# A two-layer hybrid backbone: gated expert outputs added by the scatter to the residual in DRAM, and narrow products turned round

## The chip, the cores and the metric

The kernel runs on one core of one Trainium2 chip, in fp32. The metric is the device time of one execution in microseconds. The change is judged by the median of several executions, before against after.

## What is computed

One inference step of a two-layer backbone over 640 tokens (128 context, 512 latent) of 1024 features. Layer 0 is attention beside a convolution, layer 1 a gated DeltaNet; behind each stands a hierarchical mixture of 16 experts, of which every token uses two. Each half layer is added to the residual x after multiplication by a gate row. There are two gate rows, one for context tokens and one for latent tokens. Cut to what matters here:

```python
def hier_moe(h, w_gr, b_gr, w_er, b_er, w_gate, w_up, w_down):
    t = h.reshape(b * l, d)
    g_logits = (t @ w_gr).astype(F32)                  # 4 groups
    e_logits = (t @ w_er).astype(F32)                  # 16 experts
    ...                                                # one group, two experts in it, weights e_w
    combine = jnp.sum(jax.nn.one_hot(expert, N_EXPERTS) * e_w[..., None], 1)
    hid = jax.nn.silu(jnp.einsum('td,edf->tef', t, w_gate)) * jnp.einsum('td,edf->tef', t, w_up)
    out = jnp.einsum('tef,efd->td', hid * combine[..., None], w_down)
# in the layer: x = x + gate_row * hier_moe(modulate(rms_norm(x, g), shift, scale))
# DeltaNet: proj = h @ w_in, whose last 32 columns are the gates (beta and decay)
```

## The kernel before

The five token tiles of 128 stand in SBUF as X. Five engines run their own instruction lists: PE (TensorE), DVE (VectorE), ACT (ScalarE), POOL (GpSimd) and SP, which issues the weight loads. Semaphores join them.

**Output projection and logits** (`out_pe`, `out_act`, `out_dve`, once a layer). PE projects ten half tiles (L973). From the seventh on, it also transposes the normalised rows of a tile that is ready (L985), which ACT copies to hT, and multiplies them by the 20 router columns (L992): per tile eight products with hT as the weights of 128 columns, of which only 20 columns are streamed. Each fp32 product is two instructions. POOL stores the normalised rows to h2d in DRAM.

**Routing** (`route_dve`, `route_pe`) gives each of the 1280 (token, expert) pairs a slot. There are 16 expert tiles of 128 slots and a loop over extra tiles, which runs at least once, so that 17 tiles are worked off in each layer here. The result is two index lists: tokens to gather, and rows of y2d (two rows per token) to scatter to. Free slots point at 256 padding rows.

**Experts** (`moe_*`). For tile t, POOL gathers 128 rows of h2d (L1326, 512 KB). PE transposes them (L1378), runs gate and up (L1386, 64 instructions), transposes tile t+1, and then runs down (L1397). ACT takes the silu, and DVE multiplies into the hidden tile (L1450). The down result is copied from PSUM to one of two buffers yb, half by ACT and half by DVE (L1426, `y_copy`), and POOL scatters it to y2d (L1330, 512 KB). Before each gather and each scatter POOL runs a one-column multiplication and a drain (`gate`, L1322). POOL's order is gather t+4, scatter t, gather t+5, scatter t+1, and so on, to the gather of tile 16; after that come scatters alone. The copy of tile t waits until the scatter of tile t-2 has landed, since it takes its buffer. DVE's order is hidden t, transposed rows of t+1, copy t, hidden t+1. SP loads 3 MB of weights per tile, four tiles ahead.

**Combination** (`comb_*`). When everything has landed, SP loads both rows of each token from y2d (L1475 and L1476, ten loads of 512 KB). ACT multiplies one by its weight (L1480). DVE adds the other by its weight (L1484), multiplies by the gate row (L1487) and adds to X (L1489). In layer 0 each tile then goes through the next norm: ACT squares (L1494) and takes a root, DVE scales (L421), PE transposes (L456), and ACT modulates eight 128x128 blocks (L400) into hT. Behind it `gates_pe` multiplies hT by the 32 gate columns (L1615): 40 products, 80 instructions, with 32 columns streamed. In layer 1 X is stored to the outputs (L2375).

## Time and profile before

| | us |
|---|---|
| median of 3 runs | 1771.22 |
| lowest, highest | 1764.03, 1777.72 |
| the profiled execution | 1759.8 |
| its span in the trace | 1757.9 |
| PE busy | 1476.2 (84%) |
| DVE, ACT, POOL busy | 744.2, 508.0, 178.6 |
| DMA moved | 268.09 MB, mean 153 GB/s |

The profiled execution is 11.4 us below the median. The page lists busy time by engine, by 40 slices of the span, and by groups of instructions; an idle time in a group stands with what ended it ("<-"). A row of the timeline is start, duration, engine, line, operation, output from inputs, and in brackets the idle time ahead of it and its releaser. "PEclk" is the granted TensorE clock as a share of 2.4 GHz: 1.00 is 2.4 GHz, 0.50 is 1.2 GHz. A DMA's row on POOL or SP is the time of issuing it. The time from issue to landing is listed apart.

### The profile page before, as it was taken

The numbers are of one execution on the slowest core, as the hardware profiler recorded it, in microseconds if no ns is written. First come the engines' busy times: TensorE is split into PE (matmuls) and PEld (weight loads), VectorE is DVE, ScalarE is ACT, GpSimd is POOL, SyncE is SP. The second block draws the span as 40 slices with busy tenths as digits, with TensorE's granted clock in tenths as the row PEclk, the third lists the DMA queues.
The fourth block names the chain that finished last, engine by engine and source line by source line (L and its number), as shares of the span: only waits on it lengthen the run. The fifth ranks groups of instructions, "written<-read, shape, count | busy, mean of one in ns | idle before, by whom it ended". The sixth has DMA issues, their size and how long they took to land.

```text
span 1757.9 us, 33612 instructions
## 1 busy us (share of the span) xinstructions
PE 1476.2 (84%) x14556; PEld 1070.3 (61%) x14556; DVE 744.2 (42%) x1420; ACT 508.0 (29%) x1115; POOL 178.6 (10%) x249
## 2 busy tenths in 40 slices
PE   3999669979869989368989999989989996899892
PEld 2556357754558767265767767767755445787671
DVE  0375867632421111233655556566645435111114
ACT  2202334440201101254544545445432111111011
POOL 3000020010011111102101101110100000211120
PEclk8999689999869999758988899999999996899996
DMA  9413774522469985522011112012013315698845
GB/s 359 161 51 131 243 251 149 189 63 107 172 236 329 342 294 195 208 71 62 29 42 39 39 42 58 21 42 70 5 54 130 113 72 203 227 349 295 277 173 210
DMA packets 166260, 268.09 MB, mean 153 GB/s; under 512 B 7408, under 2 KB 106912, under 8 KB 165600
## 3 DMA queue, kind: packets, MB, share of 16 engines
q1 hardware_dynamic: 150720, 210.32, 35.8%
q0 software_dynamic: 15392, 55.61, 8.6%
q8 instruction: 115, 1.88, 0.5%
q14 instruction: 33, 0.27, 0.0%
HBM read 237.93 MB, written 27.98 MB: 151 GB/s over the span
## 4 chain that ended last, share of the span: by engine, by line
PE 53%; issue 21%; DVE 9%; DMA 6%; ACT 4%; POOLq 3%; DVEq 2%; POOL 1%; SPq 0%; ACTq 0%; PEldq 0%
PE psum L1746 8%; PE psum L973 7%; PE psum L541 4%; PE psum L1808 3%; POOLq L1323 3%; DMA ring<-in_w_mod 3%; PE psum L1386 3%; PE psum L311 2%; PE psum L821 2%; PE psum L1758 2%; PE psum L2305 2%; PE psum L527 2%; PE psum L800 2%; DMA arena<-in_w_mod 1%; PE psum L1397 1%
## 5 line engine op out<-in xcount | busy, mean ns | idle before, releaser
L1746 PE MATMUL psum<-hT,ring 128*128 128x384 f32 (+1 forms) x768 | 257.0, 461 | 2.0 <-ACT modN L1976 1.6
L1746 PEld LDWEIGHTS psum<-hT,ring 128*128 128x128 f32 x768 | 136.7, 197 | 39.7 <-issue 3.9
L1386 PEld LDWEIGHTS psum<-arena,ring 128*128 128x128 f32 x1152 | 134.0, 195 | 12.0 <-issue 9.6
L1386 PE MATMUL psum<-arena,ring 128*128 128x128 f32 x1152 | 134.8, 279 | 3.7 <-DVE arena L1420 3.7
L1426 DVE COPY arena<-psum 128x512 f32<-128x512 f32 x34 | 23.5, 692 | 240.7 <-DMA y2d<-arena,small 192.3
L673 DVE SCALAR_TENSOR_TENSOR arena<-arena,params_sb 128x655 f32<-128x655 f32 x120 | 106.3, 913 | 4.8
L1808 PEld LDWEIGHTS psum<-arena 32*32 32x32 f32 x5120 | 55.8, 110 | 69.6 <-issue 41.7
L1808 PE MATMUL psum<-arena 32*32 32x32 f32 x5120 | 65.1, 200 | 32.5 <-issue 21.9
L1426 ACT COPY arena<-psum 128x512 f32<-128x512 f32 x34 | 19.9, 586 | 244.9 <-DMA y2d<-arena,small 207.5
L1397 PE MATMUL psum<-ring,arena 128*128 128x512 f32 x144 | 71.6, 644 | 15.2 <-DVE arena L1450 15.2
L1397 PE MATMUL psum<-modN,arena 128*128 128x512 f32 x128 | 60.7, 619 | 12.2 <-DVE arena L1450 12.2
L541 PE MATMUL psum<-hT,ring 128*128 128x512 f32 (+1 forms) x256 | 70.3, 435 | 0.7 <-ACT modN L604 0.7
L973 PE MATMUL psum<-ring,hT 128*128 128x512 f32 x160 | 69.6, 594 | 1.2 <-ACTq L208 1.2
L973 PE MATMUL psum<-ring,arena 128*128 128x512 f32 x160 | 69.6, 594 | 1.2 <-ACTq L208 1.2
L1450 DVE TENSOR_TENSOR arena<-arena,psum 128x256 f32<-128x256 f32 x34 | 14.3, 421 | 127.5 <-PE psum L1386 125.1
L1386 PEld LDWEIGHTS psum<-arena,hT 128*128 128x128 f32 x512 | 58.4, 192 | 3.8 <-issue 3.8
L1386 PEld LDWEIGHTS psum<-arena 128*128 128x128 f32 x512 | 58.4, 192 | 3.8 <-issue 3.8
L541 PEld LDWEIGHTS psum<-hT,ring 128*128 128x128 f32 x256 | 38.9, 191 | 32.6 <-issue 32.6
L1386 PE MATMUL psum<-arena 128*128 128x128 f32 x512 | 58.5, 275 | 0.0
L1386 PE MATMUL psum<-arena,hT 128*128 128x128 f32 x512 | 58.5, 275 | 0.0
L1397 PEld LDWEIGHTS psum<-ring,arena 128*128 128x128 f32 x144 | 28.2, 206 | 46.2 <-issue 30.3
L1032 DVE TENSOR_TENSOR arena<-psum,modG 128x512 f32<-128x512 f32 x20 | 13.8, 691 | 94.9 <-PE psum L973 94.9
(419 smaller groups left out, 2598.9 us busy)
## 6 DMA issues: line engine op xcount, KB each, us to landing
ring<-in_w_mod SPq DMA_DIRECT2D x24, 1024.0 KB, 5.3
ring<-in_m_w_gate SPq DMA_DIRECT2D x18, 1024.0 KB, 6.6
ring<-in_m_w_up SPq DMA_DIRECT2D x18, 1024.0 KB, 9.9
ring<-in_m_w_down SPq DMA_DIRECT2D x18, 1024.0 KB, 8.3
arena<-in_w_mod SPq DMA_DIRECT2D x16, 1024.0 KB, 5.4
modN<-in_m_w_down SPq DMA_DIRECT2D x16, 1024.0 KB, 9.7
ring<-in_c_w_in SPq DMA_DIRECT2D x24, 512.0 KB, 7.0
arena<-y2d SPq DMA_DIRECT2D x20, 512.0 KB, 6.9
```

What stands on the lines that cost most here:

```text
L311: m = pe.matmul(out[32 * j:32 * j + 2, :], cond[:, k, :], w[:, c0:c0 + P], start=(k == 0), stop=(k == KC - 1))
L527: m = pe.matmul(bank(t % 2, LAT), hT[:, k, tok(t)], ring[:, 0, k * LAT:(k + 1) * LAT], start=(k == 0), stop=(k == KC - 1))
L541: m = pe.matmul(out, ring[:, s, c0:c0 + P], hT[:, k, o:o + n], start=(k == 0), stop=(k == KC - 1))
L673: m = dve.scalar_tensor_tensor(out=acc[:, fc, :], in0=src, scalar=conv_w(fc, k), in1=acc[:, fc, :], op0=ALU.mult, op1=ALU.add)
L800: m = pe.matmul(bank(b, n0), qT[0:QK, h, tok(qt)], kT[0:QK, h, k0 * P:k0 * P + n0], start=True, stop=True)
L973: m = pe.matmul(bank(n % 4), lhs[:, k, tok(t)], ring[:, OUT_SLOT[l][nb], k * 512:(k + 1) * 512], start=(k == 0), stop=(k == KC - 1))
L1323: pool.drain()
L1386: m = pe.matmul(bank((2, 4)[half] + (1, 3)[half] * q, P, f * P), gu_slot[s][:, c0:c0 + P], xgT[:, q, k, :], start=(k == 0), stop=(k == KC ...
L1397: m = pe.matmul(bank(5 + nb), hidT[:, q, k, :], dn_slot[s][:, k * D + nb * 512:k * D + nb * 512 + 512], start=(k == 0), stop=(k == 1))
L1426: copy(yb[:, q, half * 512:(half + 1) * 512], bank(5 + half)).then_inc(S(f"moe{l}_y"), 1)
L1746: m = pe.matmul(bank(un % 2, w), ring[:, s, c0k:c0k + P], hT[:, k, o:o + w], start=(k == 0), stop=(k == KC - 1))
L1808: m = pe.matmul(bank(b, 32, 32 * i)[QD(q), :], lhs(5 * g + i, q), rhs(5 * g + i, q), start=True, stop=True)
```

## The change

Five things are changed.

1. The residual goes to DRAM. When X is complete ahead of the experts, SP stores it to a new tensor x2d (one DMA, 2.6 MB, on SP's queue ahead of the loads of down weights 2 and 3). The scatter of an expert tile does not write to y2d but adds to x2d (`compute_op=ALU.add`). Since a token has two experts, a scatter waits until the one before it has landed, and the first waits until X is stored.
2. The weight and the gate row move to the expert tile. Routing makes one list (the token row) and two weights per slot: one for a context token and one for a latent token, of which one is zero. DVE builds a gate tile G from the two gate rows (`gate_of`, one tensor_scalar and one scalar_tensor_tensor over 128x1024), and multiplies both halves of the down result by it from PSUM (`y_gated`). ACT has no part in it any more.
3. The combination goes. In layer 0 SP loads the five tiles of X back from x2d. In layer 1 SP copies x2d to the two outputs, DRAM to DRAM.
4. The router logits and the DeltaNet gates are turned round (`narrow_rows`): the 32 narrow columns are the weights and the 128 tokens of hT are streamed. The eight feature blocks go in turn to four groups of 32 output partitions. The result is copied to SBUF, and one product with stacked 32x32 identities adds the four groups and transposes (`logits`, `gate_columns`). The gates go in between the transposes of the next norm.
5. In that norm DVE modulates four of the eight blocks (`modulate_dve`), as it did in the first norm. Two more pad stores of 512 KB, to x2d, stand at the start of POOL's list.

```diff
             for r in range(0, NPAD, P):
                 pool.dma_start(h2d[T + r:T + r + P, :], pad[:]).then_inc(S("pad_stored"), 16)
+                pool.dma_start(x2d[T + r:T + r + P, :], pad[:]).then_inc(S("pad_stored"), 16)
...
+        def modulate_dve(dve, l, t):
+            dve.wait_ge(S("norm_tr"), l * 4 * NT + 2 * t + 2)
+            for j in range(4):
+                k, c = 4 + j, cond_of(t)
+                m = dve.tensor_scalar(hT[:, k, tok(t)], bank(2 + (2 * t + 1) % 4, P, j * P),
+                                      mcol[:, l, 1, k, c:c + 1], mcol[:, l, 0, k, c:c + 1], ALU.mult, ALU.add)
+            m.then_inc(S("in_hT_dve"), 1)
...
+        def narrow_rows(pe, out, w_of, t):
+            for k in range(KC):
+                j = k % 4
+                m = pe.matmul(out[32 * j:32 * j + 32, :], w_of(k), hT[:, k, tok(t)], start=(k < 4), stop=(k >= 4))
+            return m
...
+            def logit_rows(t):
+                pe.wait_ge(S("norm_hT"), l * 2 * NT + 2 * t + 2)
+                if t >= 1:
+                    count_wait(pe, "lg_ev", l * NT + t)
+                first = PARAM_AT["w_r"][0] + l * KC * LGC
+                w = lambda k: params[:, first + k * LGC:first + k * LGC + 32]
+                narrow_rows(pe, bank(7, P), w, t).then_inc(S("lg_mm"), 1)
             def logits(t):
-                pe.wait_ge(S("norm_hT"), l * 2 * NT + 2 * t + 2)
-                for k in range(KC):
-                    w = (l * KC + k) * LGC
-                    m = pe.matmul(bank(7, LGC, t * 32), hT[:, k, tok(t)], PRM("w_r")[:, w:w + LGC], start=(k == 0), stop=(k == KC - 1))
-                return m
+                count_wait(pe, "lg_ev", l * NT + t + 1)
+                return pe.matmul(bank(7, LGC, 256 + t * 32), rows[:, t, :], C("eye32")[:, 0:LGC], start=True, stop=True)
             for n in range(2 * NT):
                 project(n)
                 t = n - NT
                 if t >= 1:
                     h_to_features(t - 1)
+                if t >= 3:
+                    logits(t - 3)
                 if t >= 2:
-                    logits(t - 2)
+                    logit_rows(t - 2)
+            logits(NT - 3)
+            logit_rows(NT - 2)
+            h_to_features(NT - 1)
             logits(NT - 2)
-            h_to_features(NT - 1)
+            logit_rows(NT - 1)
             logits(NT - 1).then_inc(S("rt_by_pe"), 1)
...
+            def logit_copy(t):
+                count_wait(act, "lg_mm", l * NT + t + 1)
+                act.copy(rows[:, t, :], bank(7, P)).then_inc(S("lg_ev"), 1)
...
-            dve.tensor_tensor(LBx[:, :, 0, :], LBx[:, :, 2, :], rep(C("row_id"), LT, 2), ALU.mult)
-            for k in range(2):
-                m = dve.tensor_tensor(LBx[:, k * NT:(k + 1) * NT, 1, :], LBx[:, k * NT:(k + 1) * NT, 2, :], rep(C("row_id")[:, 0:NT], LT, 2), ALU.mult)
-            m.then_inc(S("rt_by_dve"), 1)
+            dve.tensor_tensor(LBx[:, :, 1, :], LBx[:, :, 2, :], rep(wk.rearrange("p k t -> p (k t)"), LT, 2), ALU.mult)
+            dve.tensor_tensor(LBx[:, :, 0, :], LBx[:, :, 2, :], rep(C("row_id"), LT, 2), ALU.mult).then_inc(S("rt_by_dve"), 1)
...
+            dve.tensor_scalar(w_cond[:, 0, :], idxf, float(SEQ), None, ALU.is_lt)
+            dve.tensor_copy(w_slot, bank(6, LT, LT))
+            dve.drain()
+            dve.tensor_tensor(w_cond[:, 0, :], w_cond[:, 0, :], w_slot, ALU.mult)
+            dve.drain()
+            dve.tensor_tensor(w_cond[:, 1, :], w_slot, w_cond[:, 0, :], ALU.subtract)
...
             sp.wait_ge(S("norm_h"), (2 * l + 2) * NT)
+            sp.dma_start(x2d[0:T, :].rearrange("(t p) d -> p t d", p=P), X[:, :, :]).then_inc(S("x_stored"), 16)
...
             def scatter(idx, q):
-                pool.indirect_dma_start(out=y2d, out_offset=bass.IndirectOffsetOnAxis(ap=idx, axis=0),
-                                        in_=yb[:, q, :], in_offset=None).then_inc(S(f"moe{l}_scattered{q}"), 16)
+                pool.indirect_dma_start(out=x2d, out_offset=bass.IndirectOffsetOnAxis(ap=idx, axis=0),
+                                        in_=yb[:, q, :], in_offset=None, compute_op=ALU.add).then_inc(S(f"moe{l}_scattered{q}"), 16)
...
                 count_wait(pool, f"moe{l}_y", 2 * (t + 1))
+                if t == 0:
+                    pool.wait_ge(S("x_stored"), 16 * (l + 1))
+                else:
+                    count_wait(pool, f"moe{l}_scattered{part(t - 1)}", 16 * ((t + 1) // 2))
                 gate()
                 scatter(rows_of(t), part(t))
...
-        def y_copy(eng, copy, l, t, q, half, scattered):
-            count_wait(eng, f"moe{l}_dn_mm", t * 2 + 1 + half)
-            if not isinstance(t, int) or t >= 2:
-                count_wait(eng, f"moe{l}_scattered{q}", scattered)
-            copy(yb[:, q, half * 512:(half + 1) * 512], bank(5 + half)).then_inc(S(f"moe{l}_y"), 1)
+        def gate_of(dve, t, w):
+            dve.tensor_scalar(G[:, 0, :], modG[:, 0, :], w[0], None, ALU.mult)
+            dve.drain()
+            dve.scalar_tensor_tensor(out=G[:, 1, :], in0=modG[:, 1, :], scalar=w[1], in1=G[:, 0, :], op0=ALU.mult, op1=ALU.add)
+            dve.drain()
+        def y_gated(dve, l, t, q, scattered):
+            for half in range(2):
+                c = slice(half * 512, (half + 1) * 512)
+                count_wait(dve, f"moe{l}_dn_mm", t * 2 + 1 + half)
+                if half == 0 and (not isinstance(t, int) or t >= 2):
+                    count_wait(dve, f"moe{l}_scattered{q}", scattered)
+                dve.tensor_tensor(yb[:, q, c], bank(5 + half), G[:, 1, c], ALU.mult).then_inc(S(f"moe{l}_y"), 1)
...
-                y_copy(act, act.copy, l, t, part(t), 0, 16 * (t // 2))
...
-                y_copy(dve, dve.tensor_copy, l, t, part(t), 1, 16 * (t // 2))
+                gate_of(dve, t, (w_cond[:, 0, t:t + 1], w_cond[:, 1, t:t + 1]))
+                y_gated(dve, l, t, part(t), 16 * (t // 2))
...
+            if l == 1:
+                for O_y, r0, n in ((O["y_prompt"][0], 0, SEQ), (O["y_sample"][0], SEQ, DEC)):
+                    sp.dma_start(O_y, x2d[r0:r0 + n, :]).then_inc(S("y_out"), 16)
+                sp.wait_ge(S("y_out"), 32)
+                return
             for t in range(NT):
-                sp.dma_start(y1[:, t, :], y2d[t * P:(t + 1) * P, :]).then_inc(S(f"cb_y{t}"), 16)
-                sp.dma_start(y2[:, t, :], y2d[T + t * P:T + (t + 1) * P, :]).then_inc(S(f"cb_y{t}"), 16)
-        def comb_weigh(act, l, t):
-            count_wait(act, f"cb_y{t}", 32 * (l + 1))
-            act.mul(y1[:, t, :], y1[:, t, :], wk[:, 0, t:t + 1]).then_inc(S("cb_w1"), 1)
-        def comb_add(dve, l, t):
-            dve.wait_ge(S("cb_w1"), l * NT + t + 1)
-            dve.scalar_tensor_tensor(out=y2[:, t, :], in0=y2[:, t, :], scalar=wk[:, 1, t:t + 1], in1=y1[:, t, :],
-                                     op0=ALU.mult, op1=ALU.add)
-            dve.drain()
-            dve.tensor_tensor(y2[:, t, :], y2[:, t, :], modG[:, cond_of(t), :], ALU.mult)
-            dve.drain()
-            dve.tensor_tensor(X[:, t, :], X[:, t, :], y2[:, t, :], ALU.add).then_inc(S("cb_used"), 1)
+                sp.dma_start(X[:, t, :], x2d[t * P:(t + 1) * P, :]).then_inc(S(f"cb_y{t}"), 16)
...
-                act.wait_ge(S("cb_used"), t + 1)
+                count_wait(act, f"cb_y{t}", 16)
                 act.activation(junk[:], X[:, t, :], ACT.Square, accum_out=ss[:, t:t + 1])
                 act.drain()
                 act.activation(rstd[:, t:t + 1], ss[:, t:t + 1], ACT.Sqrt, scale=1.0 / D, bias=C("eps")).then_inc(S("norm_rms"), 1)
             for t in range(NT):
-                comb_weigh(act, 0, t)
-            for t in range(NT):
                 square(t)
                 if t >= 1:
-                    for half in range(2):
-                        modulate_act(act, 1, t - 1, half)
-            for half in range(2):
-                modulate_act(act, 1, NT - 1, half)
+                    modulate_act(act, 1, t - 1, 0)
+            modulate_act(act, 1, NT - 1, 0)
...
+            def gate_copy(t):
+                count_wait(dve, "gt_mm", t + 1)
+                dve.tensor_copy(grows[:, t, :], bank(t % 2, P)).then_inc(S("gt_ev"), 1)
             for t in range(NT):
-                comb_add(dve, 0, t)
                 if t >= 1:
                     scale(t - 1)
+                if t >= 2:
+                    modulate_dve(dve, 1, t - 2)
+                if t >= 3:
+                    gate_copy(t - 3)
             scale(NT - 1)
+            modulate_dve(dve, 1, NT - 2)
+            gate_copy(NT - 3)
+            modulate_dve(dve, 1, NT - 1)
+            gate_copy(NT - 2)
+            gate_copy(NT - 1)
...
         def gates_pe(pe):
-            pe.wait_ge(S("g1_w"), 16)
+            def gate_rows(t):
+                if t == 0:
+                    pe.wait_ge(S("g1_w"), 16)
+                pe.wait_ge(S("in_hT_act"), NT + t + 1)
+                pe.wait_ge(S("in_hT_dve"), NT + t + 1)
+                if t >= 2:
+                    count_wait(pe, "gt_ev", t - 1)
+                narrow_rows(pe, bank(t % 2, P), lambda k: ring[:, 2, k * 32:(k + 1) * 32], t).then_inc(S("gt_mm"), 1)
+            def gate_columns(t):
+                count_wait(pe, "gt_ev", t + 1)
+                return pe.matmul(bank(6, 32, t * 32), grows[:, t, :], C("eye32"), start=True, stop=True)
             for t in range(NT):
-                pe.wait_ge(S("in_hT_act"), NT + 2 * t + 2)
-                for k in range(KC):
-                    m = pe.matmul(bank(0, 32, t * 32), hT[:, k, tok(t)], ring[:, 2, k * 32:(k + 1) * 32], start=(k == 0), stop=(k == KC - 1))
-            m.then_inc(S("g1_by_pe"), 1)
+                norm_tile_pe(pe, 2, t)
+                if t >= 3:
+                    gate_columns(t - 3)
+                if t >= 1:
+                    gate_rows(t - 1)
+            arrive(pe, "pe")
+            gate_columns(NT - 3)
+            gate_rows(NT - 1)
+            gate_columns(NT - 2)
+            gate_columns(NT - 1).then_inc(S("g1_by_pe"), 1)
```

What PE runs between the experts of layer 0 and the heads, before (L456 transposes, L1615 gate products, L1620 cumulative sums):

```order
L456 MATMUL psum<-consts_sb,hbuf 128x128 x40
L1615 MATMUL psum<-ring,hT 128x32 x40
L1620 MATMUL psum<-small,consts_sb 128x8 x10
L1621 MATMUL psum<-small,consts_sb 128x80
L1624 MATMUL psum<-consts_sb,small 80x128
```

and now (L457 transposes, L968 turned products, L1661 the product with the identities):

```order
L457 MATMUL psum<-consts_sb,hbuf 128x128 x16
L968 MATMUL psum<-hT,ring 32x128 x8
L457 MATMUL psum<-consts_sb,hbuf 128x128 x8
L968 MATMUL psum<-hT,ring 32x128 x8
L457 MATMUL psum<-consts_sb,hbuf 128x128 x8
L1661 MATMUL psum<-consts_sb,arena 128x32
L968 MATMUL psum<-hT,ring 32x128 x8
L457 MATMUL psum<-consts_sb,hbuf 128x128 x8
L1661 MATMUL psum<-consts_sb,arena 128x32
L968 MATMUL psum<-hT,ring 32x128 x8
L1661 MATMUL psum<-consts_sb,arena 128x32
```

The gate products have moved in between the transposes; behind the last transposes (those of tile 4) only tile 4's own products and three small ones are left.

What DVE runs for two expert tiles, before (L1450 hidden, L1420 transposed rows, L1426 its half of the copy):

```order
L1450 TENSOR_TENSOR arena<-arena,psum 128x256
L1420 COPY arena<-psum 128x512
L1426 COPY arena<-psum 128x512
L1450 TENSOR_TENSOR arena<-arena,psum 128x256
L1420 COPY arena<-psum 128x512
L1426 COPY arena<-psum 128x512
```

and now (L1497 hidden, L1460 rows, L1464 and L1466 the gate tile, L1475 both halves):

```order
L1497 TENSOR_TENSOR arena<-arena,psum 128x256
L1460 COPY arena<-psum 128x512
L1464 TENSOR_SCALAR arena<-modG,small 128x1024
L1466 SCALAR_TENSOR_TENSOR arena<-modG,small,arena 128x1024
L1475 TENSOR_TENSOR arena<-psum,arena 128x512 x2
L1497 TENSOR_TENSOR arena<-arena,psum 128x256
```

The gate tile and the second half have come in ahead of the next hidden tile.

What SP issues ahead of the experts of layer 0 now:

```order
L1298 DMA arena<-in_m_w_gate 128x8x256
L1299 DMA arena<-in_m_w_up 128x8x256
L1336 DMA x2d<-resid 128x5x1024
L1302 DMA modN<-in_m_w_down 128x2x1024 x2
L1298 DMA hT<-in_m_w_gate 128x8x256
L1299 DMA hT<-in_m_w_up 128x8x256
```

The third row is new; the rest stands as before.

## Rows read from the trace of the kernel before

**Rows 1.** Busy time by stretch: engines' busy us (instructions), PEclk, DMA share, GB/s
```profile
0.00:50.00 50.00, 19.40 (x291) 14.26 (x292) 7.64 (x21) 13.95 (x29) 13.33 (x25) 0.87 0.98 362
...
496.00:505.00 9.00, 2.03 (x10) 1.81 (x9) 0.80 (x4) 0.00 (x0) 3.22 (x5) 0.50 0.24 66
...
550.00:573.00 23.00, 23.00 (x163) 19.17 (x163) 3.61 (x6) 3.11 (x6) 3.25 (x6) 1.00 1.00 347
...
670.00:695.00 25.00, 22.80 (x161) 18.94 (x160) 3.53 (x7) 2.81 (x6) 4.79 (x8) 1.00 0.60 209
```

**Rows 2.** Timeline of POOL in the experts of layer 0
```profile
523.18 1.00 POOL L1330 DMA_INDIRECT y2d<-arena,small  x1 [0.89 <-issue]
...
531.43 0.98 POOL L1326 DMA_INDIRECT arena<-h2d,small  x1 [7.02 <-issue]
...
539.97 1.00 POOL L1330 DMA_INDIRECT y2d<-arena,small  x1 [6.23 <-issue]
...
685.02 1.00 POOL L1330 DMA_INDIRECT y2d<-arena,small  x1 [6.47 <-issue]
```

**Rows 3.** Issue to landing: scatters at 523, at 540, from 700; gather at 513
```profile
DMA to landing us min/median/max: 7.5/7.5/7.5
...
DMA to landing us min/median/max: 8.9/8.9/8.9
...
DMA to landing us min/median/max: 3.3/3.3/4.5
...
DMA to landing us min/median/max: 4.4/4.4/4.4
```

**Rows 4.** Timeline of the experts of layer 0 near 612, all engines
```profile
611.74 0.69 DVE L1426 COPY arena<-psum 128x512 f32<-128x512 f32 x1 [12.99 <-DMA y2d<-arena,small]
...
613.11 5.40 PE L1397 MATMUL psum<-ring,arena 128*128 128x512 f32 x8 [3.63 <-DVE arena L1450]
```

**Rows 5.** Timeline of the combination of layer 0, the norm and the gates
```profile
728.90 0.35 SPq L1475 DMA_DIRECT2D arena<-y2d  x1
...
733.83 1.15 ACT L1480 ACTIVATE arena<-arena,small 128x1024 f32<-128x1024 f32 x1 [11.82 <-DMA arena<-y2d]
...
742.14 1.15 ACT L1480 ACTIVATE arena<-arena,small 128x1024 f32<-128x1024 f32 x1 [1.42 <-DMA arena<-y2d]
...
749.56 1.28 DVE L1484 SCALAR_TENSOR_TENSOR arena<-arena,small 128x1024 f32<-128x1024 f32 x1
...
763.02 1.09 ACT L1494 ACTIVATE junk<-resid 128x1024 f32<-128x1024 f32 x1
...
764.96 5.70 ACT L400 ACTIVATE hT<-psum,small 128x128 f32<-128x128 f32 x16 [0.40 <-PE psum L456]
...
767.71 14.65 PE L1615 MATMUL psum<-ring,hT 128*128 128x32 f32 x80 [0.26 <-issue]
...
782.47 0.29 ACT L1629 COPY small<-psum 128x160 f32<-128x160 f32 x1 [11.81 <-PE psum L1615]
```

**Rows 6.** Timeline of the combination of layer 1, to the end
```profile
1725.42 0.99 POOL L1330 DMA_INDIRECT y2d<-arena,small  x1 [0.76 <-issue]
...
1729.43 0.34 SPq L1475 DMA_DIRECT2D arena<-y2d  x1
...
1753.57 1.23 DVE L1489 TENSOR_TENSOR resid<-resid,arena 128x1024 f32<-128x1024 f32 x1
```

**Rows 7.** Timeline of the logits of tiles 1 and 4 in layer 0
```profile
457.43 1.86 PE L992 MATMUL psum<-params_sb,hT 128*128 128x20 f32 x16
...
475.02 3.60 PE L992 MATMUL psum<-params_sb,hT 128*128 128x20 f32 x16 [0.68 <-ACT hT L1013]
```

**Rows 8.** Busy time by stretch, where only L311 or L992 runs on PE
```profile
34.30:38.00 3.70, 3.61 (x65) 2.28 (x66) 0.00 (x0) 0.00 (x0) 0.00 (x0) 0.50 1.05 386
41.00:43.00 2.00, 1.79 (x64) 1.45 (x56) 0.00 (x0) 0.15 (x1) 0.00 (x0) 1.00 1.06 381
...
475.00:479.00 4.00, 3.60 (x16) 3.49 (x16) 0.35 (x2) 1.26 (x1) 0.00 (x0) 0.50 1.08 382
```

103 lines of the change are left out of this document (44 added, 59 removed).

## The prediction

> **What bounds the kernel now.** I read the table by stretch first, then the timelines of the stages that the change touches, and then the list of landings.
>
> The experts take some 220 us a layer. At first PE sets the pace: it is busy for all of 550 to 573, and DMA is full too (share 1.00, 347 GB/s) [rows 1]. But look at POOL in the same stage [rows 2]. The scatter issued at 523.18 lands 7.5 us later, at 530.7, and the gather behind it is issued at 531.43. That gather is followed by the scatter of 539.97, which takes 8.9, and so on. POOL issues each of these transfers about 0.8 us after the one before has landed, so they form one serial chain, gather and scatter in turn. On full DMA a pair costs about 16 us, while PE needs 11.5 for a tile (23.0 busy for two in 550 to 573). So the scatters fall behind, by 4 to 5 us a tile. Near tile 9 the buffer of the result is missing: DVE waits 13.0 us for a scatter at 611.74, and PE waits 3.6 for DVE at 613.11 [rows 4]. From there to the last gathers POOL's chain sets the pace. From the scatter of tile 0 (523.18) to that of tile 12 (685.02) it takes 161.8 us, 13.5 a tile. The chain eases itself as it slows the weights down: the DMA share falls to 0.60 in 670 to 695 [rows 1], and a scatter on a free queue takes 3.3 [rows 3].
>
> The two combinations are bare: PE has nothing to do in them. In layer 0, 53.6 us go by from the first load of y2d (728.90) to the end of the gate products (782.47), 14.65 of them in 80 narrow instructions [rows 5]. In layer 1 it is 28.5 us from 1729.43 to the end of the span at 1757.9 [rows 6].
>
> **Start (+2.9).** Two pad stores more, 1.05 MB, at the 362 GB/s of a stage that is DMA-bound (share 0.98) [rows 1]. The other end is 0, if the loads that PE waits for land ahead of them.
>
> **Logits (-3.7 a layer, -7.3).** Now 16 instructions take 1.86 us at 2.4 GHz, and 3.60 for the last tile at 1.2 GHz [rows 7, 8]. The nearest rows to the turned form are the modulation products, with two columns as weights, 128 streamed, and the four groups of output partitions in turn: about 1.9 us for 64 at 2.4 GHz and 3.6 at 1.2 [rows 8], so 0.48 and 0.9 for 16. Ends for ours, with 32 columns as weights: 0.48, and the old 1.86. I take 0.6 and 1.1, nearer to the modulation rows since the streamed length and the groups are theirs. The closing product adds an eighth of the old time, 0.23 or 0.45. Ahead of the last projection 3.7 become 1.4 (two turned sets, one closing product). At the last tile 3.60 become 1.1 + 0.45 + an ACT copy of 0.3 (as L1629) with 0.4 for its two hand-overs, 2.25. Sum 2.3 + 1.35. Other end: 1.5 lost a layer.
>
> **Combination of layer 0 (-28).** The loads now come in pairs from 733.83 on, three pairs later at 742.14 [rows 5], that is 1.4 us each. So X's first tile lands at 732.4 and all by 738. Then ACT paces. A tile costs a square and a root (763.02 to 764.96 less 0.4 waiting, 1.5) and four modulations (5.70 / 16 each, 1.4), with waits 3.1 [rows 5]. DVE has less, since its three passes of 1.2 to 1.3 are gone and four small modulations come in. Allow 3 for tile 0 and four tiles of 3.1: 747.8. Then scaling 1, transposes 2, modulations 1.4, turned products 1.1, copy and closing product 1.1: 754.4. Against 782.47 that is -28. If the 32 columns cost as much as the old form (PE's clock is low here), PE paces at 6 a tile and the term is -16. The head weights queue behind five loads in place of ten on SP, and the gate arithmetic that follows is unchanged.
>
> **End (-18).** Two DRAM-to-DRAM copies, 2.6 MB. A first 512 KB takes 3.5 us (728.90 to 732.4), and the other four 1.4 each: 9.1. If reading and writing DRAM add up, 14.7 and a bit. I take 10.5, nearer to the loads since each byte still passes one DMA engine once: 28.5 - 10.5 = 18; ends -19 and -13.
>
> **Store of X (+1 a run).** 2.6 MB ahead of down weights 2 and 3, 7 us of full DMA. The DMA share is 0.24 in 496 to 505 [rows 1], so the store pushes its tail into that gap. The first gathers, 4 us earlier than now, may meet it. Ends 0 and 3. The weights behind it are used two tiles later.
>
> **DVE in the experts (0).** The gate tile is two passes of at most 1.28 [rows 5], built while PE runs down, and DVE has 11.5 us a tile for some 5. After a late scatter both halves go one after the other on DVE (0.7 more), but ACT's silu is then done already. Cover gone, it would be 0.5 a stalled tile, some 5 in all. The new wait for the scatter before costs nothing: POOL already waits for it in [rows 2].
>
> **The adding scatter (+13 a layer, and +1.8 at each layer's end: +29.6).** No row shows one. It must read 512 KB of DRAM besides what it does now. Below, 0: the read goes beside the read of SBUF. Above, a whole gather more: 4.4 on a free queue [rows 3], and 7.7 on a full one (531.43 to 539.97, less 0.8) [rows 2]. I take +1.8: the bytes alone are 1.4, and a gather lands 1.1 later than a scatter on a free queue (4.4 against 3.3) for reading DRAM instead of SBUF, of which I count part. That is nearer to the bytes than to a whole gather, since issue, write and receipt are there already. POOL's chain has 12 scatters from tile 0 to 12: 21.6 a layer if nothing gives way. I take 60% of it, 13, because the lag first has to use up its slack, and because slower tiles empty the DMA queue (8.9 falls to 3.3). The last scatter of each layer is bare: 1.8 twice.
>
> **Sum.** 2.9 - 7.3 - 28 - 18 + 1 + 29.6 = -19.8, from the profiled execution's 1759.8 to 1740. The median of the runs is 11.4 higher, so against 1771.2 the forecast is 1751.
>
> **The rivals.**
> (a) The scatter costs nearly nothing more, at most 0.8: 12 x 0.8 x 0.6 a layer, twice, and 1.6, together 13. 1771 - 49.4 + 13 = 1735. For it: reads of SBUF and DRAM can overlap. Against it: the chain shows every us of landing.
> (b) The second read doubles the byte part of each scatter. That part is 1.4 of 3.3 on a free queue, and grows to about 6 of 8.9 on a full one [rows 3]. With 4 as the mean it is 12 x 4 = 48 a layer, of which the emptier queue gives back half: 25 a layer, and 1.4 twice at the ends, 53. 1771 - 49.4 + 53 = 1775, no change. The Trainium skill, Collectives: The Full Stack, section "The bandwidth ceiling: the fold count and why AG ≠ RS ≠ AR", holds that the add itself is free but needs two source reads on one ring, and so runs at about half the rate of a copy. By that rule the time is 1775. No run here shows an adding transfer yet.
> (c) Slower: reading and writing a row do not overlap, and each scatter costs a gather more, 7.7 on full DMA: 92 a layer, half given back, 46, and 4.4 at each end: 101. 1771 - 49.4 + 101 = 1823. It decides against the change from about 2.8 us more per scatter on (12 x 0.65 x 2 + 2 = 17.6 us per us, against 49.4). For it: POOL's chain hides nothing.
> (d) The turning does not do what it says: 32 columns cost as much as 128. The logits lose 3 instead of gaining 7.3, the combination gains 16. 1751 + 10 + 12 = 1773.
>
> **How the numbers follow.** My forecast, 1736 to 1766: 0.36. (a) 0.24, (b) 0.14, (c) 0.18, (d) 0.08. One per cent, 17.7 us, is about what a measurement of this kernel can tell from no change. The bound is 1753.5. Faster: (a) and 0.20 of the forecast, 0.44. Within: 0.16 of it, 0.10 of (b) and (d), 0.34. Slower: (c) and 0.04 of (b), 0.22. The range from 1725 to 1806 leaves out a small part of (a), and the upper two thirds of (c). The forecast's own range is 1736 to 1766.
>
> **What would show it.** Landings of the adding scatter: near 5 on a free queue, 9 to 11 on a full one. POOL's steps from tile 0 to 12: about 14.6 a tile. PE's wait for hidden tiles starts before tile 9, near tile 6 or 7. The turned products: 16 instructions in 0.5 to 0.7 us at 2.4 GHz. From the first load of x2d to the copy of the gates: 25 us. From the first output copy to the end: 10 to 11. What would make it wrong is the scatter's price above all: each us of it is worth 17 us.

## The result, and the profile after

The changed kernel takes 1774.55 us (median of 20 runs, 1766.52 to 1783.32). The kernel before takes 1761.71 over its 20 runs (the 1771.22 of the table above came from three of them). The ratio is 1.0074, with a 95% interval of 1.0053 to 1.0094: slower by 13 us, inside the one per cent that I called no change. The forecast, 1751 and faster, was wrong, and by more than the two times show: it stood on a base of 1771.2, 9.5 above the median of 20. As a change it was -20, and +13 was measured. The profiled executions are 1757.9 (before) and 1779.0 (after), 21.1 apart, and this difference can be followed stage by stage. All figures of the table are in us, read from the two timelines.

| Stage | Before | After | Difference | Predicted |
|---|---|---|---|---|
| start of the kernel to the first input product | 52.3 | 54.2 | +1.9 | +2.9 |
| input, attention of layer 0 (not changed) | 338.1 | 340.4 | +2.2 | 0 |
| output projection and logits, layer 0, layer 1 | 88.2, 88.5 | 86.4, 84.5 | -1.9, -4.1 | -3.7, -3.7 |
| routing to the first tile of an expert, layer 0, layer 1 | 26.8, 26.7 | 27.6, 26.7 | +0.8, 0 | +1 in sum |
| experts, first transposes to last down product | 217.6, 221.4 | 243.3, 242.0 | +25.6, +20.5 | +13, +13 |
| bare end, last down product to SP's next issue | 5.9, 5.9 | 13.3, 14.6 | +7.4, +8.7 | +1.8, +1.8 |
| combination of layer 0, norm, gate products | 53.6 | 22.6 | -30.9 | -28 |
| gate arithmetic, heads, z1 of layer 1 (not changed) | 604.4 | 612.7 | +8.3 | 0 |
| end of layer 1 | 28.5 | 11.0 | -17.5 | -18 |

The small terms and the two large gains came out within 3 us. The two lines in the middle did not: the experts and their bare ends cost 62 us together, where I had 30. The heads lost 8.3 us without any change to their work. Cut into eight stretches of 69 us, PEclk is lower there in three (0.85, 0.93 and 0.95, against 0.98, 1.00 and 0.98), higher in one (0.95 against 0.87), and within 0.01 in the other four. No experiment was made for it, but the profiles of the experiments below settle most of it. From the copy of the gates to the last product of layer 1's routing, the changed kernel and eleven of the experiments run the same number of instructions on PE (8617), on ACT (691), and on DVE but for one (885 or 886). It took them from 695.6 us at a mean PEclk of 0.96 (the fifth experiment) to 716.5 at 0.92 (the changed kernel). So the loss in the heads is of the size that the clock alone makes between profiles, and in a stretch as long as this one a difference of 10 us between two profiles says nothing by itself.

These are the stretches of [rows 1] in the kernel after (engines' busy us with their instructions, then PEclk, DMA share, GB/s):

```profile
496.00:505.00 9.00, 4.20 (x20) 3.98 (x19) 2.59 (x15) 0.00 (x0) 1.73 (x3) 0.50 1.06 378
550.00:573.00 23.00, 23.00 (x163) 19.17 (x163) 8.70 (x12) 1.94 (x4) 5.31 (x6) 1.00 1.03 314
670.00:695.00 25.00, 21.79 (x132) 16.62 (x133) 7.53 (x11) 1.35 (x3) 5.94 (x8) 0.93 0.65 183
```

PE is still busy for all of 550 to 573. The store of X fills the gap at 496 that [rows 1] had at 0.24, and it costs at most the 0.8 us that the first tile of layer 0 comes later. DVE has gone from 3.6 to 8.7 of 23, still far from full. POOL in the same experts, which answers to [rows 2]:

```profile
526.39 1.61 POOL L1365 DMA_INDIRECT x2d<-arena,small  x1 [0.89 <-issue]
...
535.69 1.01 POOL L1361 DMA_INDIRECT arena<-h2d,small  x1 [7.45 <-DMA x2d<-arena,small]
...
544.82 2.02 POOL L1365 DMA_INDIRECT x2d<-arena,small  x1 [7.86 <-issue]
...
704.50 1.60 POOL L1365 DMA_INDIRECT x2d<-arena,small  x1 [5.26 <-issue]
...
720.40 1.60 POOL L1365 DMA_INDIRECT x2d<-arena,small  x1 [3.88 <-issue]
...
727.98 1.90 POOL L1365 DMA_INDIRECT x2d<-arena,small  x1 [0.85 <-issue]
...
736.39 1.57 POOL L1365 DMA_INDIRECT x2d<-arena,small  x1 [1.06 <-issue]
...
744.16 1.56 POOL L1365 DMA_INDIRECT x2d<-arena,small  x1 [0.82 <-issue]
...
752.23 1.02 POOL L1361 DMA_INDIRECT arena<-h2d,small  x1 [0.80 <-issue]
...
758.17 1.60 POOL L1365 DMA_INDIRECT x2d<-arena,small  x1 [0.75 <-issue]
```

Here a slip of mine has to be put right: the scatters of 685.02 in [rows 2] and of 704.50 here are the twelfth, of tile 11, and I had taken them for tile 12's. (The expectations below repeat it.) From tile 0 to tile 11 the chain takes 178.1 us, 16.2 a tile, and before it was 161.8, 14.7 a tile. All of the 16.3 between them is in the landings of the scatters: the eleven of tiles 0 to 10, read one by one, add up to 65.5 us before and 82.2 after, while the eleven gathers between them took 78.9 and 78.6. In the tail behind tile 12 the scatters follow each other at 8 us, where the kernel before had 4 to 5. Landings of the adding scatter: the one at 526.39, the one at 544.82, and the five from 720 on, to be read beside [rows 3]:

```profile
DMA to landing us min/median/max: 8.5/8.5/8.5
...
DMA to landing us min/median/max: 10.3/10.3/10.3
...
DMA to landing us min/median/max: 6.2/6.4/7.0
```

The first two, on a full queue, land 1.0 and 1.4 later than the plain ones (7.5, 8.9), those on a free queue 3.1 later (3.3). PE's wait begins two tiles before that of [rows 4], which by the count of down products is for tile 8, and not for tile 9:

```profile
591.38 1.29 DVE L1475 TENSOR_TENSOR arena<-psum,arena 128x512 f32<-128x512 f32 x2 [10.30 <-DMA x2d<-arena,small]
593.05 5.35 PE L1437 MATMUL psum<-modN,arena 128*128 128x512 f32 x8 [3.27 <-DVE arena L1497]
```

DVE's gated copy of tile 5 waits 10.3 us for a scatter, the hidden tile 6 that PE needs is queued behind it on DVE, and PE waits 3.3. The bare end of layer 0, POOL and SP:

```profile
750.83 0.18 POOL L1390 COPY small<-small 128x1 int32 x1 [4.88 <-issue]
...
751.73 0.69 DVE L1475 TENSOR_TENSOR arena<-psum,arena 128x512 f32<-128x512 f32 x1 [0.54 <-PE psum L1437]
...
756.83 0.18 POOL L1397 COPY small<-small 128x1 int32 x1 [3.36 <-issue]
...
764.57 0.19 POOL L1357 TENSOR_TENSOR small<-consts_sb 128x1 f32<-128x1 f32 x1 [4.57 <-DMA x2d<-arena,small]
764.98 2.47 SPq L1535 DMA_DIRECT2D resid<-x2d  x5
```

The last gated half is ready at 752.4. But POOL is late. Its scatter of tile 15 landed at about 750.6, the gather behind it went out at 752.23, and only after that one's landing comes the last scatter, at 758.17. In the kernel before, the gather in this place was issued at 717.21 and landed before the last down product ended at 723.02. So nothing stood ahead of the last scatter, which went out 1.9 us after that end. Now it is 6.5.

One more row is worth its place. It is the drain that stands in `gate()`, ahead of every transfer of POOL (a drain is written to hold an engine until what it started is done): first of the kernel before, then of the kernel after (count, then ns min/median/max):

```profile
L1323 POOLq DRAIN  x72: 271/5117/9630, 499.2 to 1729.0; - x72
```

```profile
L1358 POOLq DRAIN  x72: 262/6600/11292, 501.3 to 1767.6; - x72
```

An empty drain takes 0.27 us. The median one takes 5.1, and 6.6 after the change: about as long as a transfer is under way. The waits that I had read as "POOL issues each transfer 0.8 us after the one before has landed" [rows 2] have this instruction in them. Two single ones of the kernel before:

```profile
L1323 POOLq DRAIN  x1: 7733/7733/7733, 523.0 to 523.0; - x1
...
L1323 POOLq DRAIN  x1: 9189/9189/9189, 539.8 to 539.8; - x1
```

The first ends at 530.7, where the scatter issued at 523.18 lands (7.5 later). The second ends at 549.0, where that of 539.97 has landed (8.9 later, 548.9).

### The profile page after: what moved, and what is told of

Same layout as the page of the kernel before. It is cut to its first block, busy times and chain, and to the rows that moved or that the text cites. A ratio compares the mean times of both kernels' runs of the same rounds, so it can differ in the third digit from the quotient of the medians.

```text
span 1779.0 us, 33785 instructions
## 1 busy us (share of the span) xinstructions
PE 1479.3 (83%) x14586; PEld 1060.1 (60%) x14586; DVE 798.8 (45%) x1527; ACT 474.0 (27%) x1061; POOL 206.1 (12%) x251
## 4 chain that ended last, share of the span: by engine, by line
PE 47%; issue 25%; DVE 8%; DMA 7%; POOLq 5%; ACT 4%; DVEq 2%; POOL 2%; ACTq 0%; SPq 0%
PE psum L1803 8%; PE psum L983 7%; POOLq L1358 4%; PE psum L542 4%; PE psum L1865 3%; DMA ring<-in_w_mod 3%; PE psum L312 2%; DMA x2d<-arena,small 2%; PE psum L822 2%; PE psum L1815 2%; PE psum L2362 2%; PE psum L528 2%; PE psum L801 1%; DMA arena<-in_w_mod 1%; DVE modN L2180 1%
## 5 line engine op out<-in xcount | busy, mean ns | idle before, releaser
L1803 PEld LDWEIGHTS psum<-hT,ring 128*128 128x128 f32 x768 | 138.2, 199 | 39.4 <-issue 4.5
L1426 PEld LDWEIGHTS psum<-arena,ring 128*128 128x128 f32 x1152 | 138.8, 201 | 16.2 <-issue 13.7
L1475 DVE TENSOR_TENSOR arena<-psum,arena 128x512 f32<-128x512 f32 x68 | 44.2, 687 | 228.3 <-DMA x2d<-arena,small 225.7
L1426 PE MATMUL psum<-arena,ring 128*128 128x128 f32 x1152 | 139.6, 285 | 7.9 <-DVE arena L1460 7.9
L1437 PE MATMUL psum<-modN,arena 128*128 128x512 f32 x128 | 70.2, 699 | 34.8 <-DVE arena L1497 34.8
L1480 ACT ACTIVATE arena<-psum 128x256 f32<-128x256 f32 x34 | 13.0, 383 | 307.8 <-PE psum L1426 307.8
L1365 POOL DMA_INDIRECT x2d<-arena,small x34 | 56.4, 1658 | 162.5 <-issue 162.5
L1437 PEld LDWEIGHTS psum<-modN,arena 128*128 128x128 f32 x128 | 27.3, 224 | 67.3 <-DVE arena L1497 37.6
L1460 ACT COPY arena<-psum 128x512 f32<-128x512 f32 x34 | 19.9, 585 | 175.6 <-PE psum L1418 175.6
L1426 PEld LDWEIGHTS psum<-arena 128*128 128x128 f32 x512 | 58.4, 192 | 3.9 <-issue 3.9
L1426 PEld LDWEIGHTS psum<-arena,hT 128*128 128x128 f32 x512 | 58.4, 192 | 3.8 <-issue 3.8
L2342 POOL TENSOR_TENSOR arena<-arena,consts_sb 128x640 f32<-128x640 f32 x8 | 12.3, 1541 | 413.5 <-PE psum L1915 405.3
L1497 DVE TENSOR_TENSOR arena<-arena,psum 128x256 f32<-128x256 f32 x34 | 14.1, 416 | 101.4 <-PE psum L1426 101.4
L1426 PE MATMUL psum<-arena,hT 128*128 128x128 f32 x512 | 58.5, 275 | 0.0
```

The costliest lines, as they stand in the source:

```text
L1365: pool.indirect_dma_start(out=x2d, out_offset=bass.IndirectOffsetOnAxis(ap=idx, axis=0), in_=yb[:, q, :], in_offset=None, compute_op=ALU.a ...
L1426: m = pe.matmul(bank((2, 4)[half] + (1, 3)[half] * q, P, f * P), gu_slot[s][:, c0:c0 + P], xgT[:, q, k, :], start=(k == 0), stop=(k == KC ...
L1437: m = pe.matmul(bank(5 + nb), hidT[:, q, k, :], dn_slot[s][:, k * D + nb * 512:k * D + nb * 512 + 512], start=(k == 0), stop=(k == 1))
L1475: dve.tensor_tensor(yb[:, q, c], bank(5 + half), G[:, 1, c], ALU.mult).then_inc(S(f"moe{l}_y"), 1)
L1803: m = pe.matmul(bank(un % 2, w), ring[:, s, c0k:c0k + P], hT[:, k, o:o + w], start=(k == 0), stop=(k == KC - 1))
```

## Experiments

My theory was: the adding scatter lands later by more than its bytes, and since a drain makes every transfer of POOL wait for the one before, the whole of it shows in the chain. The rivals were that DVE's gating, the store of X or the new wait is what costs, and that the order comes from the queue itself.

**1. Adding taken away (e1).**

```diff
-  in_=yb[:, q, :], in_offset=None, compute_op=ALU.add)
+  in_=yb[:, q, :], in_offset=None)
```

> The changed kernel with scatters that overwrite instead of adding: the output of an expert replaces the token's row, so the sum over experts and residual is left out. All else is the same: DVE's gates and gated copies, the store of X, POOL's waits, the short combination. If the add itself is the cost (my theory): a scatter lands in about 3.3 us on a free queue instead of 6.6, POOL issues it in 1.0 us instead of 1.6, the experts take 218 to 222 us a layer (243 and 242 now), the bare ends fall from 13.3 and 14.6 to about 6 and 7, and the run takes about 1775 - 46 - 14 = 1715 us. If the store of X, the wait for the scatter before, or the work moved from ACT to DVE is the cost: the experts stay near 240 us a layer and the run near 1765 to 1775.

Measured: 1743.5 us, ratio to before 0.9871 (0.982 to 0.9921). Layer 1 isn't the same work here: with other values the routing made 35 tiles in all instead of 34. So its experts took 246.0, of which 24.6 lie behind the last down product of the 17th tile (1705.43 to 1729.99); the first 17 took 221.4. Less that, the run would be near 1719. In layer 0 the work is the same. The experts took 227.4 (243.3 with adding, 217.6 before), the bare end 5.8 (13.3), and the five last scatters landed so:

```profile
L1365 POOL DMA_INDIRECT x2d<-arena,small x5: 971/984/991, 712.1 to 738.5; - x5
...
DMA to landing us min/median/max: 3.3/3.3/3.4
```

The store of X, the waits and DVE's gating are all still in. The add itself is 16 of the 26 us in layer 0, all of the 20.5 in layer 1 (242.0 to 221.4), and all of the bare end. The 227.4 of layer 0 is above the 218 to 222 of the expectation; the 10 us that are left there are judged by the fourth and fifth experiments.

**2 and 3. The drain taken away, after and before (e2, e3).** In the 16 unrolled tiles the small product, which carries the wait, writes a column of its own, so no drain is needed behind it:

```diff
+            def gate(drain=True):
...
+                else:
+                    pool.tensor_tensor(at(15600 + next(gates), 1), ident[:, 0:1], ident[:, 0:1], ALU.mult)
...
-                gate()
+                gate(False)
                 scatter(rows_of(t), part(t))
```

> The changed kernel; in the 16 unrolled tiles of a layer the small product ahead of each POOL transfer writes a column of its own and has no drain behind it (the loop over further tiles keeps its drain). If the drain makes POOL wait until its outstanding transfer has landed (theory A): a gather is issued while the scatter before it is still under way, POOL's chain from tile 0 to tile 12 falls from 178 us to about 150 to 165, the experts to 225 to 235 a layer, and the run takes 1745 to 1765 us. The wait of a scatter for the scatter before remains, with a gather between them. If POOL's order comes from the queue itself or from the waits on other engines (rival): POOL's issues stay about 0.8 us behind the landing before, and the run takes 1770 to 1778 us.

> The kernel before with the same edit as in e2_after_nodrain: no drain behind the small product ahead of each POOL transfer in the 16 unrolled tiles. Theory A (the drain waits for the landing): the chain of 161.8 us from tile 0 to 12 falls to 140 to 150, PE's waits for hidden tiles go from 57 us towards 20, and the run takes 1735 to 1755 us against 1762. Rival (order from queue or other waits): 1758 to 1765 us.

Measured on the same chip: 1688.0 for the changed kernel (ratio to before 0.9592, 0.9549 to 0.9635) and 1723.7 for the kernel before (0.9789, 0.9751 to 0.9827). Both gained more than theory A had asked for. The experts took 201.4 and 201.9 us in the one, 201.6 and 201.2 in the other. The changed kernel's POOL:

```profile
526.62 1.62 POOL L1369 DMA_INDIRECT x2d<-arena,small  x1 [0.15 <-issue]
...
528.63 1.01 POOL L1365 DMA_INDIRECT arena<-h2d,small  x1 [0.15 <-issue]
...
538.08 1.61 POOL L1369 DMA_INDIRECT x2d<-arena,small  x1 [0.15 <-issue]
...
540.07 1.00 POOL L1365 DMA_INDIRECT hbuf<-h2d,small  x1 [0.15 <-issue]
...
DMA to landing us min/median/max: 8.6/9.4/10.7
```

The gather now goes out 2.0 us behind the scatter, while that one is under way for 9.4. A tile takes 11.46 us, PE's own pace. PE's waits for hidden tiles are 1.2 us in layer 0, from 27.2, and in the kernel before 1.2, from 13.9 (the 57 of the expectation counts PE's products and weight loads, in both layers). The queue takes a second transfer at once, so the rival is out. The edit also gives each product a column of its own, but the single drains above end with the landings, so the wait is the drain's. What the add still costs is at the bare ends, 10.7 and 10.2 against 5.9 and 5.9. And the change, which loses 13 us with the drain, gains 36 without it.

**4. The narrow products alone, on the kernel before (e4).** The diff's parts on `narrow_rows`, `logit_rows`, `gate_rows` and `modulate_dve`, with y2d and both combinations kept:

```diff
+                if t >= 2:
+                    modulate_dve(dve, 1, t - 2)
+                if t >= 3:
+                    gate_copy(t - 3)
```

> The kernel before with one part of the change alone: the narrow products of router and gates turned round, with the modulation of layer 1 shared between ACT and DVE and the products moved into the combination. y2d, the plain scatters and both combinations stay. In the changed kernel the logits saved 1.9 and 4.1 us. If the turned products also explain a good part of the 31 us that the combination of layer 0 lost (my view: without them PE needs some 3 us a tile for them, with ACT's modulations ahead), the combination and its products fall from 53.6 to 36 to 42 us and the run takes 1736 to 1748 us. If the 31 us came from the missing combination passes and loads (rival), the stage stays at 48 us or more and the run takes 1750 to 1757 us.

Measured: 1744.6 us, ratio 0.9867 (0.9823 to 0.991), 21 us less than before. The combination with its products took 45.2 us (736.14 to 781.35). This lies between the two expectations. The turned products and the shared modulation give 8 of the 31 us there, and DVE paces what is left:

```profile
762.12 1.27 DVE L1514 SCALAR_TENSOR_TENSOR arena<-arena,small 128x1024 f32<-128x1024 f32 x1
...
763.47 1.23 DVE L1517 TENSOR_TENSOR arena<-arena,modG 128x1024 f32<-128x1024 f32 x1
764.77 1.23 DVE L1519 TENSOR_TENSOR resid<-resid,arena 128x1024 f32<-128x1024 f32 x1
...
768.29 1.27 DVE L1514 SCALAR_TENSOR_TENSOR arena<-arena,small 128x1024 f32<-128x1024 f32 x1
```

It needs 6.2 us a tile with its three passes, the scaling and the modulations. The experts took 225.3 in layer 0 and 219.6 in layer 1, although nothing in them was changed against the 217.6 and 221.4 before. So a chain that is held by the drain can vary by some 8 us with no change in it, and the 10 us left open in experiment 1, absent in its layer 1, are little more than that. What made them was not found.

**5. Gating on DVE, with plain scatters (e5).** The changed kernel with y2d, without the store of X and the wait for the scatter before, and with a combination of two passes:

```diff
+            dve.tensor_tensor(y2[:, t, :], y2[:, t, :], y1[:, t, :], ALU.add)
+            dve.drain()
+            dve.tensor_tensor(X[:, t, :], X[:, t, :], y2[:, t, :], ALU.add).then_inc(S("cb_used"), 1)
```

> The changed kernel with its scatter turned back: outputs of experts are gated on DVE and the narrow products are turned as in the changed kernel, but plain scatters go to y2d, there is no store of X, and a combination X + y1 + y2 of two DVE passes a tile stays in both layers. If the move of the gated copies to DVE costs nothing and the adding scatter is what slows the experts (my theory): experts 216 to 222 us a layer, bare ends about 6, combination of layer 0 about 33 to 38, end of layer 1 25 to 28, and the run takes 1725 to 1740 us. If DVE's gating is what slows the experts: 230 us or more a layer, scatters landing as in the kernel before, and the run takes 1755 us or more.

Measured: 1728.6 us, ratio 0.9785 (0.976 to 0.9811). Experts 224.0 and 221.2, bare ends 5.8 and 5.8, combination of layer 0 32.0, end 22.5. This is what my theory had, with layer 0 2 us above its range and the combination and the end below theirs. So DVE's gating costs nothing that stands out from the spread of experiment 4, and this part of the change is a gain. The one part that turns 1729 into 1775 is the adding scatter into X in DRAM, with its store and its wait, with the drain in place; experiment 1, which keeps store and wait, shows that it is the add.

**6, 7 and 8. What adding is priced by (e6a, e6b, e9).** Half of the rows, adding and plain, and half of the columns, adding (the changed arguments alone; each kernel leaves out half of every expert's output, so only layer 0 is read):

```diff
-  IndirectOffsetOnAxis(ap=idx, axis=0),       in_=yb[:, q, :]
+  IndirectOffsetOnAxis(ap=idx[0:64], axis=0), in_=yb[0:64, q, :]
```

```diff
-  out=x2d,                                       in_=yb[:, q, :]
+  out=x2d.rearrange("r (a b) -> (r a) b", a=2),  in_=yb[:, q, 0:D // 2]
```

> The changed kernel, whose scatters add the first 64 rows of each tile alone (256 KB in place of 512); the rest of the expert outputs is left out, so routing in layer 1 is another and only layer 0 is read. If the price of adding is in bytes (a second read), a landing on a free queue falls from 6.1 to about 3.6 to 4, and its issue row on POOL stays near 1.6. If it is a fixed latency of an adding transfer, it stays above 5. By descriptors made on POOL (rival), the issue row falls from 1.6 to about 1.1.

> As e6a_add_half, but the 64 rows overwrite instead of adding. Free landings: 3.3 for 128 rows of a plain scatter; for 64 rows about 2.6 if 1.4 us of them are bytes, and 1.9 or less if nearly all of it is bytes or descriptors. The difference of the two kernels gives the price of adding 64 rows: about 1.4 if it goes by bytes, about 2.8 if it is fixed.

> The changed kernel with its drains, whose adding scatters move 128 rows of 2 KB (half of the columns, 256 KB) in place of 64 rows of 4 KB as in e6a_add_half; the rows go to the wrong places and half of each expert output is left out, so only layer 0 is read. Adding cost 1.3 us more than a plain scatter for 64 rows and 2.8 for 128 rows of 4 KB. If it goes by bytes, a free landing is again 4.5 to 4.8 us; if it goes by rows (each row's read and write in turn), it is about 6.1 as for whole rows. POOL's issue row, 1.60 for 128 rows and 1.41 to 1.46 for 64, stays near 1.60 if it goes by rows.

The five last scatters of layer 0 on a free queue, in this order: adding 64 rows, plain 64 rows, adding 128 half rows (the issue row in ns, then the landing):

```profile
L1365 POOL DMA_INDIRECT x2d<-arena,small x5: 1410/1421/1473, 704.4 to 735.4; - x5
...
DMA to landing us min/median/max: 4.5/4.6/4.7
```

```profile
L1365 POOL DMA_INDIRECT x2d<-arena,small x5: 892/915/1892, 704.1 to 731.7; - x5
...
DMA to landing us min/median/max: 3.2/3.3/4.2
```

```profile
L1365 POOL DMA_INDIRECT x2d<-arena,small x5: 1562/1579/1605, 709.2 to 741.6; - x5
...
DMA to landing us min/median/max: 4.6/4.8/4.9
```

A plain scatter takes 3.3 us for 64 rows (256 KB) as for 128 (512 KB): on a free queue its bytes don't show. Adding costs 1.3 more for 64 rows, 3.1 for 128, and 1.5 for 128 half rows, if a plain scatter of these takes 3.3 too, which no run shows. So of the three prices in the expectations bytes fit best, a fixed one or one by rows does not. The landing of 64 rows, 4.6, is between what the expectation of e6a has for bytes (3.6 to 4) and for a fixed price (above 5), since it took part of the plain time for bytes. The issue row on POOL hardly depends on the rows (1.42 for 64, 1.58 to 1.60 for 128), so it isn't halved as the rival of descriptors made on POOL would have it.

**9 to 12. Is the adding scatter worth it without the drain?** Experiment 5's kernel without the drain (e7), the changed kernel without it and with one drain in the loop (e8, again as e11), and e7 with the same loop (e10). The edit of the loop:

```diff
+                count_wait(pool, f"moe{l}_scattered1", i * 16 + 16 * ((NS + 1) // 2))
+                gate()
                 pool.tensor_copy(gidx, idx_i[:, bass.ds(i + (NS + 1), 1)])
+                pool.tensor_copy(sidx, idx_i[:, bass.ds(i + NS, 1)])
                 pool.drain()
```

> The kernel of e5_gated_plain (gated on DVE, plain scatters to y2d, a short combination in both layers) without the drain of e2_after_nodrain. It is to be held against e2_after_nodrain, which took 1688 us with the adding scatter. If adding costs nothing once POOL's transfers may overlap (my theory: PE paces the experts at 201 to 202 us a layer in both), the adding kernel is ahead by what its shorter combination and end save less 4.6 us at each bare end: 32.0 to 22.8 in layer 0 and about 23 to 11 in layer 1, 21 us less 9, so this kernel takes about 1700 us (1695 to 1705). If adding still holds up the experts somewhere the profile of e2 doesn't show (rival): 1688 us or less.

> The kernel of e2_after_nodrain, and in the loop over further tiles both indices are copied ahead of the gather, with one drain, so that nothing waits between the gather and the last scatter. In e2 the last gated half is ready at 711.64 and the last scatter is issued at 714.29, behind a drain that waited for the gather of 707.79. If that drain holds it: the scatter is issued about 0.8 us behind the last gated half, the bare ends fall from 10.7 and 10.2 to about 8.5, and the run takes 1680 to 1686 us against 1688. If the loop's registers or the wait for the scatter of tile 15 hold it: no change, 1686 to 1690.

> The kernel of e7_gated_plain_nodrain (plain scatters, short combinations, no drain) with the loop's one drain of e8_best. It is held against e11_best_again, which has adding scatters, on the same chip. In the profiles of the pair e7 and e2 the adding kernel was ahead by 9.5 us in the combination of layer 0 and 12.2 at the end, and behind by 4.9 and 3.7 at the bare ends, 13 in sum; over separate calls the medians, 1691 and 1688, showed 3 of it. If the profiles' sum is right, this kernel takes 10 to 15 us more than e11. If adding costs the other stages what the profile puts down to the clock (rival), the two are within 4 us.

> The kernel of e8_best once more (adding scatters, no drain in the unrolled tiles, one drain in the loop), beside e10_plain_loop on the same chip. By the profiles it takes 10 to 15 us less than e10_plain_loop; by the rival the two are within 4 us. Against the kernel before the ratio is 0.951 again, within 0.004.

Measured: e7 1691.1 (ratio 0.9573, 0.9527 to 0.9619), 4 below the expected range. Against e2, taken on another chip, nothing can be told from that, since the intervals overlap. The pair on one chip tells it: e10 1693.9 (0.9599, 0.9552 to 0.9646) and e11 1681.8 (0.9534, 0.9485 to 0.9583), 12 us apart, as the profiles' sum had it. The ratios' intervals touch, but no run of e10 (1688.3 to 1699.4) is as fast as the slowest of e11 (1687.2), and between the gates' copy and layer 1's routing their profiles are alike (710.7 and 711.4). e8, the same kernel as e11, took 1674.0 (0.9511, 0.947 to 0.9552), 6 below its expected range. The experts of e7 took 202.8 and 201.3, against 201.6 and 201.2 in e3: without the drain the gating on DVE costs 1.2 us at the most. The loop's part was seen as meant: the last scatter now goes out behind the last gated half.

```profile
708.79 0.20 POOL L1362 TENSOR_TENSOR arena<-consts_sb 128x1 f32<-128x1 f32 x1 [2.71 <-DVE arena L1477]
709.13 1.60 POOL L1369 DMA_INDIRECT x2d<-arena,small  x1
...
715.96 0.20 POOL L1359 TENSOR_TENSOR small<-consts_sb 128x1 f32<-128x1 f32 x1 [5.00 <-DMA x2d<-arena,small]
```

The bare ends fell from 10.7 and 10.2 (e2) to 8.65 and 8.3 (8.6 and 8.3 in e11). That is 4 us. With plain scatters they are 5.2 and 5.6 (e10), so the add still costs about 3 us at each end. The median fell by 14 in e8 and by 6 in e11, on three chips, so no more than the 4 us is put down to the edit. This version is the fastest, 4.9% (e8) and 4.7% (e11) below the kernel before.

## Why the prediction was wrong

**Start, logits, combination, end, store of X, DVE in the experts: right.** They were to give -49.4 and gave -51.7 (the logits of layer 0 gave half of their 3.7). The turned products took 0.65 us at 2.4 GHz and 1.08 at 1.2 (0.6 and 1.1 taken), from the first load of x2d to the copy of the gates 22.6 passed (25 taken), from the first output copy to the end 11.0 (10.5 taken). The combination was right in sum, but not in its split: I had put PE's 14.65 in [rows 5] in the middle of it, and experiment 4 shows that turning the products without dropping the passes gives only 8 of the 31. DVE's passes would have been the next limit.

**The adding scatter: the mechanism right, the size wrong.** The mechanism was a later landing that shows in POOL's chain. Of its signs came PE's wait near tile 6, landings of 8.5 and 10.3 on a full queue (9 to 11 listed), and steps longer by 1.5 a tile (1.1 listed). The landing on a free queue, near 5 by my list, did not: it was 6.4. What failed:

- *The price, "the bytes alone are 1.4".* I took the 1.4 us between two paired loads for a cost of bytes, and counted part of a gather's 1.1 on top, 1.8 in all. In the chain this was near, 1.5 a scatter (65.5 to 82.2 for eleven). But the derivation doesn't hold, since the bytes of a plain scatter don't show on a free queue (experiments 1 and 7), and there the price is 3.1, which counts in the tail and at the ends.
- *"I take 60% of it".* Nothing was given back in the chain: its landings grew by 16.7 us and it grew by 16.3.
- *The count, "12 scatters from tile 0 to 12".* It was 11 steps, to tile 11, and they account for 16.3 us of layer 0 (161.8 to 178.1), near my 13, since one step too many and the 60% worked against each other. Another 9.2 came behind tile 11: from its scatter to the end of the last down product it was 38.0 us (685.02 to 723.02), and is 47.2 (704.50 to 751.69). The queue is free there and each scatter lands 3.1 later; the scatter of tile 15 goes out 12.5 us later than before, counted from tile 11's, and slack takes only 3.3 of it. I had left the tail out.
- *The bare end, "+1.8 at each layer's end".* I priced the last scatter alone. From its issue to SP's next one it takes 2.8 and 3.0 more than before (6.8 and 7.0 against 4.0 in [rows 5, 6]). The other 4.6 and 5.7 come from what stands ahead of it: the scatter of tile 15, and the gather, which used to be over in time. A chain that is late ends late by all of its lag, not by one link.

With the measured terms, 46.1 for the experts and 16.1 for the ends, the sum is 62.2 where I had 29.6, 32.6 more. The profiles differ by 21.1 where the sum had -19.8, which is 41 apart. The other 8 are 10.5 in stages that the change doesn't touch, where the clock differed, less 2.3 of the other terms.

**Rival (b) was near by luck.** That the second read doubles the byte part came out at 1775, where the kernel is. But that is on the base of 1771; as a change it was +4, and +13 was measured. And its working isn't borne out: there was no byte part to double, and its terms for the bare ends, 1.4 each, were as far off as mine. It was close because its 25 a layer happened to be near the measured 26 and 20. The Trainium skill (Collectives: The Full Stack, section "The bandwidth ceiling: the fold count and why AG ≠ RS ≠ AR") has, for collectives on a ring, the add free and the rate halved by the second read. No run here moved an adding transfer by itself that is long enough to show a rate. What they show is that the time of one scatter of 512 KB is set otherwise: a plain one by something that isn't its bytes, an adding one by bytes as well.

**The step that was missing.** Under [rows 2] I stated that POOL waits for each landing, and took this as given. I didn't ask which instruction makes it wait. It was the drain of a gate, and it decides the sign: with it the change loses 13 us, without it the change gains 36, and the adding scatter costs the experts nothing (201.4 us against 201.6) and the bare ends 4 to 5 us each.

## What to carry to other kernels

Before a transfer's latency is put into a sum, find the instruction that makes the next one wait for it: here a drain behind a one-column product, 5 us in the median, which cost the kernel before 37 us and the changed one some 87 (on different chips). Count a serial chain to its very end, with the lag that it hands over to the bare stretch behind it. And where a change is to be refused or kept for a cost, test it with that cost's cause removed too: the order of the two versions can turn round.

## What was not expected of the hardware

- A drain on POOL lasts until the transfers that POOL has issued have landed (to 530.7 and 549.0, with landings at 530.7 and 548.9): 0.27 us where none is under way, 5.1 and 6.6 in the median here, up to 11.3. Without it two transfers run side by side, 2.0 us apart in issue, landing 9.4 and 8.9 us after it.
- A plain indirect scatter lands in 3.3 us on a free queue, whether it moves 256 or 512 KB. An adding one takes 4.6 to 4.8 for 256 KB, and 6.4 for 512.
- Its issue row on POOL is 1.60 us against 0.99, and it hardly falls with the rows (1.42 and 0.92 for 64).
- The store of X (2.6 MB, SP's queue) took 19.6 us to land in layer 0, and the first tile of the experts came 0.8 us later. In layer 1 it landed in 13.1 us, and the first tile was not later.
- The same PE instructions between two points of the kernel took 695.6 us at a mean granted clock of 0.96, and 716.5 at 0.92.
